# One stage for the reload and the first latent states, states between z products, row groups by halves at a tile's end

## What is computed

```python
def ssd_scan(xh, bm, cm, dt_raw, a_log, dt_bias, h0, reverse, with_output):
    dt = jax.nn.softplus(dt_raw + dt_bias.reshape(SSD_GROUPS, SSD_HPG))
    a_cum = jnp.cumsum(dtc * a, axis=2)
    decay_to_end = jnp.exp(a_cum[:, :, -1:] - a_cum)
    states = jnp.einsum("bcsgn,bcsgrp->bcgrpn", bc, (decay_to_end * dtc)[..., None] * xc)
    h = chunk_decay * h + states            # chunk after chunk

def peer(h, w_q, sub_keys, u_tab, v_tab):
    # per token and head: the 16 best of 128 x 128 experts, with softmax gates
    act = jax.nn.gelu(jnp.einsum("tkd,td->tk", u_tab[it], xt))
    return jnp.einsum("tk,tkd->td", gt * act, v_tab[it])
```

## Time and profile before

| | us |
|---|---|
| median of 3 runs | 4668.28 (4664.34 to 4676.31) |
| the profiled execution | 4667.22, its span 4665.4, mean granted clock of PE 0.865 |
| context peer, first to last dots | 391.9 to 1149.7 |
| reload; first latent states; outputs begin | 1161.7; 1211.9; 1242.3 |
| latent peer of layer 0 | 1456.8 to 2852.6 |
| projection of layer 1; its states; outputs begin | 2863; 3009.0; 3033.0 |
| last peer | 3335.3 to 4651.9 |

### The profile page before, as it was taken

How to read it: one execution, slowest core, us unless ns; L and a number is a source line. 1 busy time by engine, 2 the same in 40 slices (tenths; PEclk the granted TensorE clock), 3 DMA queues, 4 the chain that set the end, 5 groups by cost and what they waited for, 6 DMA issues and landing times. The chain is left out here.

```text
span 4665.4 us, 48881 instructions
## 1 busy us (share of the span) xinstructions
PE 3434.4 (74%) x15768; PEld 1728.3 (37%) x15768; DVE 3191.9 (68%) x6618; ACT 1543.8 (33%) x3799; POOL 2058.5 (44%) x1555
## 2 busy tenths in 40 slices
PE   7898889897799886555777557888997555655554
PEld 6586224332575333111333114767632111111111
DVE  5465887664766767766766776686666677777775
ACT  4442344343442225222222323474222222222221
POOL 0173444543123554555444551034355555555554
PEclk9899999999899989777789788999998777777778
DMA  5647999999647999999999995263699999999998
GB/s 212 218 158 298 410 410 395 420 423 393 232 161 272 422 417 398 409 421 421 398 425 425 391 412 211 101 204 109 236 423 413 416 412 423 414 408 414 411 418 361
DMA packets 276276, 1622.97 MB, mean 348 GB/s; under 512 B 47074, under 2 KB 61218, under 8 KB 87717
## 3 DMA queue, kind: packets, MB, share of 16 engines
q0 software_dynamic: 184320, 1342.26, 69.6%
q1 hardware_dynamic: 91700, 277.59, 16.3%
HBM read 1598.40 MB, written 21.33 MB: 347 GB/s over the span
## 5 line engine op out<-in xcount | busy, mean ns | idle before, releaser
L2727 PE MATMUL banks<-arena 128*64 128x512 f32 x5120 | 1569.3, 748 | 1003.2 <-ACT arena L2483 1001.8
L2193 POOL DMA_INDIRECT arena<-in_experts,arena x1280 | 1527.0, 1193 | 1660.0 <-PE banks L2727 1408.3
L2316 DVE CUSTOM_DVE_ANT_0 arena<-arena,token_copies 128x1024 f32<-128x1024 f32 x1280 | 1638.4, 1297 | 741.7 <-DMA arena<-in_experts,arena 681.6
L2727 PEld LDWEIGHTS banks<-arena 128*64 128x64 f32 x5120 | 377.1, 163 | 1983.4 <-ACT arena L2483 1357.0
L2476 ACT ACTIVATE arena<-arena 128x2 f32<-128x2 f32 x640 | 131.2, 205 | 1747.2 <-DVE arena L2316 1746.1
L2483 ACT ACTIVATE arena<-arena 128x64 f32<-128x64 f32 x1280 | 376.0, 340 | 298.8 <-POOL arena L2014 257.9
L303 POOL TENSOR_TENSOR wide_low<-wide_blocks,wide_high 128x1024 fp32r<-128x1024 f32 x88 | 219.1, 2513 | 277.7 <-ACT wide_high L292 233.3
L2540 PE MATMUL banks<-arena,wide_blocks 128*128 128x512 f32 (+3 forms) x960 | 307.0, 467 | 3.5 <-ACT arena L2345 2.1
L1025 POOL TENSOR_TENSOR arena<-arena 128x1024 f32<-128x1024 f32 x20 | 43.3, 2191 | 530.4 <-POOLq L853 479.5
L2617 PE MATMUL banks<-arena,wide_blocks 128*128 128x512 f32 x576 | 277.2, 619 | 0.0
L347 PE MATMUL banks<-activation_a,wide_high 128*128 128x256 f32 (+1 forms) x768 | 255.9, 333 | 23.8 <-DVE arena L1462 10.4
(11 more groups left out here) (268 smaller groups left out, 4789.0 us busy)
## 6 DMA issues: line engine op xcount, KB each, us to landing
wide_blocks<-in_wide SPq DMA_DIRECT2D x186, 1024.0 KB, 6.0
arena<-cum_rows SPq DMA_DIRECT2D x80, 256.0 KB, 3.8
arena<-in_experts,arena POOLq DMA_INDIRECT x1280, 11.1
pre_scan<-arena SPq DMA_DIRECT2D x16, 256.0 KB, 7.3
arena<-pre_scan SPq DMA_DIRECT2D x16, 256.0 KB, 5.2
residual<-in_tokens SPq DMA_DIRECT2D x6, 512.0 KB, 6.4
arena<-mod_rows SPq DMA_DIRECT2D x6, 512.0 KB, 8.5
norm_rows<-in_keys SPq DMA_DIRECT2D x3, 1024.0 KB, 6.5
```

Of the source, the lines that this page charges most:

```text
L2193: pool.indirect_dma_start(out=v.ring[:, g % RING], out_offset=None, in_=io["experts"], in_offset=bass.IndirectOffsetOnAxis(ap=c.idx[:, u % ...
L2316: last = nc.vector.tensor_tensor_reduce(out=u_row, in0=u_row, in1=k.copies[:, n % NJ], scale=1.0, scalar=0.0, op0=ALU.mult, op1=ALU.add, a ...
L2727: mm = nc.tensor.matmul(k.ps[j * QUAD:(j + 1) * QUAD, a + half], v.lhs[:, g % 4, j], v.ring[:, (g * NJ + j) % RING, D + half * BANK:D + (h ...
```

## The change

**Reload and states become one stage,** `stage_reload_states`. The modulation products come in two rounds of four. DVE's order becomes biased, box 0, steps, boxes 1 and 2, rests, joins 0 and 1, box 3, weights, joins 2 and 3, then state 0, joins 4 and 5, state 1, joins 6 and 7, states 2 to 5. PE has state(n) and modulation products between its mixes. The z rows are loaded near the end, and the first gate of the outputs stage waits for them. Buffers move to make room.

**`stage_project` has `inside=True` for layer 1's latent tokens:** dt products after product 1, the fold after 3, the decay sums after 9, their transposes after 13, the other decay steps between convolutions; the six states run after each of the first six z products; the unit decays stand behind the last z silu. `stage_states(1, LATENT)` is gone.

**In the peer stages** the last unit of a tile (but not of the stage) and the first unit of the next have their 16 rows in another order: the eight rows of half 0, then the eight of half 1. That is 14 units at seven boundaries. The next tile's copies for half 0 are made after the fourth pair of the last unit, those for half 1 after the eighth.

```diff
+            if inside:
+                load_wides(k, sp, w0 + 8 + WIDE_SLOTS)
+                sp.wait_ge(k.cum_moved.sem, k.cum_moved.at(1))
+                sp.dma_start(io["cum"].rearrange("t r c -> r t c")[:, 0:NT], cum_rows).then_inc(k.cum_kept.sem, 16)
+                sp.wait_ge(k.cum_kept.sem, kept0 + 16)
+                for n in range(4):
+                    load_sums(k, sp, after, n, 0, 0, n)
...
+                if inside and m == 1:
+                    dt_products()
+                if inside and m == 3:
+                    dt_fold()
+                if inside and m == 9:
+                    decay.sums(pe)
+                if inside and m == 13:
+                    turn_sums()
+            if not inside:
+                dt_products()
...
+                if n < len(steps):
+                    state(n)
+            if inside:
+                pe.wait_ge(k.state_added.sem, k.state_added.at(len(steps)))
+                products_bc(k, v, 0, 6)
...
+                if inside and m == 2:
+                    move_dt()
+                if inside and m == 4:
+                    copy_dt()
+                if inside and m == 6:
+                    decay.logs(act)
+                if inside and m == 12:
+                    decay.decays(act)
...
+            if inside:
+                act.wait_ge(k.cum_turned.sem, k.cum_turned.at(1))
+                nc.scalar.copy(cum_rows, k.ps[0:32, 6, 0:T].rearrange("p (t c) -> p t c", t=NT)).then_inc(k.cum_moved.sem, 1)
+            else:
...
+            if inside:
+                for n in range(EARLY_UNITS):
+                    unit_decays(k, act, after, n, 0, 0, n, row0)
...
+                if inside and m == 5:
+                    dve.wait_ge(k.dt_copied.sem, k.dt_copied.at(1))
+                    decay.biased(dve)
+                if inside and m == 7:
+                    decay.steps(dve)
+                if inside and m == 10:
+                    decay.rests(dve)
+                if inside and m == 13:
+                    decay.weights(dve)
...
+            if inside:
+                dve.wait_ge(k.turn_copied.sem, k.turn_copied.at(X_TILES + B_TILES))
+                dve.drain()
+                scale_x(0)
+                cut(9)
+                dve.wait_ge(k.silu_done.sem, k.silu_done.at(SCAN_TILES))
+                for n in range(len(steps)):
+                    state(n)
+                    if n in (1, 3):
+                        cut(10 + n // 2)
+                return
...
-            for m in range(8):
-                sp.dma_start(sig[:, m], io["pre_gp"][m]).then_inc(k.reloaded[3].sem, 16)
+            gate_rows(0)
+            gate_rows(1)
             for m in range(B_TILES):
                 sp.dma_start(v.CT[:, m], io["pre_scan"][X_TILES + B_TILES + m]).then_inc(k.reloaded[2].sem, 16)
-            for b in range(4):
-                for pair in range(2):
-                    sp.dma_start(v.zs[:, 2 * pair:2 * pair + 2, b * WIDE:(b + 1) * WIDE],
-                                 io["pre_z"][2 * b + pair].rearrange("p (t c) -> p t c", t=2)).then_inc(k.reloaded[2].sem, 16)
-            def store(m):
-                sp.wait_ge(k.part_ready.sem, k.part_ready.at(m + 1))
-                sp.dma_start(io["pre_part"][m], part[:, m % 2]).then_inc(k.part_kept[m % 2].sem, 16)
-
-            for m in range(8):
-                store(m)
-            sp.wait_ge(k.reloaded[2].sem, C + 16 * (B_TILES + 8))
+            mods.load(sp, 0)
+            wides(1)
+            sp.wait_ge(k.cum_moved.sem, k.cum_moved.at(1))
+            sp.dma_start(io["cum"].rearrange("t r c -> r t c")[:, 0:NT], cum_rows).then_inc(k.cum_kept.sem, 16)
+            store(0)
+            store(1)
+            gate_rows(2)
+            gate_rows(3)
+            wides(2)
+            wides(3)
+            sp.wait_ge(k.cum_kept.sem, kept0 + 16)
+            sp.wait_ge(k.mixed_ready.sem, k.mixed_ready.at(4))
+            for m in range(4, 8):
+                gate_rows(m)
+            for n in range(4):
+                load_sums(k, sp, v, n, 0, 0, n)
+            store(2)
+            store(3)
+            wides(4)
+            wides(5)
+            store(4)
+            store(5)
+            mods.keep(sp, 0)
+            mods.load(sp, 1)
+            z_rows(0)
+            store(6)
+            store(7)
             for i in range(2):
                 sp.wait_ge(k.part_kept[i].sem, k.part_kept[i].at(64))
+            z_rows(1)
+            wides(count)
+            mods.keep(sp, 1)
...
+            mods.take(act, 0)
             decay.decays(act)
+            act.wait_ge(k.cum_turned.sem, k.cum_turned.at(1))
+            nc.scalar.copy(cum_rows, k.ps[0:32, 5, 0:SEQ].rearrange("p (t c) -> p t c", t=NT)).then_inc(k.cum_moved.sem, 1)
+            for i in range(1, count + 1):
+                mods.take(act, i)
+                if i == 4:
+                    act.wait_ge(k.yp_proj.sem, k.yp_proj.at(8))
+                    unit_decays(k, act, v, 0, 0, 0, 0, row0)
+                if i == 5:
+                    unit_decays(k, act, v, 1, 0, 0, 1, row0)
...
+            box(0)
+            decay.steps(dve)
+            box(1)
+            box(2)
+            decay.rests(dve)
+            join(0)
+            join(1)
+            box(3)
+            decay.weights(dve)
+            join(2)
+            join(3)
+            dve.wait_ge(k.turn_copied.sem, k.turn_copied.at(X_TILES))
+            dve.drain()
+            scale_x(0)
+            state(0)
+            join(4)
+            join(5)
+            state(1)
             join(6)
             join(7)
...
+    def row_of(u, n):
+        border = (u % PEER_HEADS == 0 and u) or (u % PEER_HEADS == PEER_HEADS - 1 and u < UNITS - 1)
+        return (n % RANKS, n // RANKS) if border else (n // NJ, n % NJ)
+
+    def first_of_half(u, n):
+        return all(row_of(u, x)[1] != row_of(u, n)[1] for x in range(n))
+
+    def last_of_half(u, n):
+        return all(row_of(u, x)[1] != row_of(u, n)[1] for x in range(n + 1, TOPK))
...
-    copy_at = lambda n: FIRST + 13.0 + 3.0 * n if n < 2 * NJ else dot_at(n // (2 * NJ) * PEER_HEADS * TOPK - 1) + 5.0
+    copy_at = lambda n: (FIRST + 13.0 + 3.0 * n if n < 2 * NJ else
+                         dot_at(n // (2 * NJ) * PEER_HEADS * TOPK - 1 - (RANKS if n // 2 % NJ == 0 else 0)) + 5.0)
...
-                            in_offset=bass.IndirectOffsetOnAxis(ap=c.idx[:, u % 4, n // NJ, n % NJ:n % NJ + 1], axis=0),
+                            in_offset=bass.IndirectOffsetOnAxis(ap=row_index(u, n), axis=0),
...
-                        if u % PEER_HEADS == 0 and n < NJ:
-                            dve.wait_ge(k.copy_ready.sem, k.copy_ready.at(t * 2 * NJ + 2 * n + 2))
+                        j = row_of(u, n)[1]
+                        if u % PEER_HEADS == 0 and first_of_half(u, n):
+                            dve.wait_ge(k.copy_ready.sem, k.copy_ready.at(t * 2 * NJ + 2 * j + 2))
...
-                            out=u_row, in0=u_row, in1=k.copies[:, n % NJ], scale=1.0, scalar=0.0,
+                            out=u_row, in0=u_row, in1=k.copies[:, j], scale=1.0, scalar=0.0,
...
-                            act.wait_ge(k.dots.sem, b0["dots"] + t * PEER_HEADS * RANKS)
+                            act.wait_ge(k.dots.sem, b0["dots"] + t * PEER_HEADS * RANKS - (RANKS // 2 if j == 0 else 0))
...
-                    if u % PEER_HEADS == PEER_HEADS - 1 and t + 1 < NT:
-                        yield from copies(t + 1)
+                        if u % PEER_HEADS == PEER_HEADS - 1 and t + 1 < NT and q % (RANKS // 2) == RANKS // 2 - 1:
+                            yield from copies(t + 1, [q // (RANKS // 2)])
...
+                                n = q * NJ + j
+                                part = row_of(u, n)[1]
                                 mm = nc.tensor.matmul(
-                                    k.ps[j * QUAD:(j + 1) * QUAD, a + half], v.lhs[:, g % 4, j],
+                                    k.ps[part * QUAD:(part + 1) * QUAD, a + half], v.lhs[:, g % 4, j],
                                     v.ring[:, (g * NJ + j) % RING, D + half * BANK:D + (half + 1) * BANK],
-                                    start=(first and q == 0), stop=(final and q == RANKS - 1), skip_group_check=True)
+                                    start=(first and first_of_half(u, n)), stop=(final and last_of_half(u, n)),
+                                    skip_group_check=True)
...
+                        if final and t + 1 < NT and q == RANKS // 2 - 1:
+                            yield from copies(t + 1, [0])
...
-                            yield from copies(t + 1)
+                            yield from copies(t + 1, [1])
```

295 lines of the change are left out of this document (222 added, 73 removed).

## The result

| | us |
|---|---|
| median before / after, 4 runs each | 4668.23 / 4699.43 |
| ratio, 95% interval | 1.0075 [1.0058, 1.0093] |
| the profiled execution after | 4707.19, its span 4705.2, mean granted clock of PE 0.878 |
| forecast | 4650.0, range 4630 to 4674 |

The account below looks back on a forecast made before the run. Peer stages, two thirds of the span, were taken as bound by DMA gathers with PE in the loop, DVE or PE bounding between them. Terms -7 - 9 - 2 = -18 on 4667.2 give 4649.2, median 4650, range 4630 to 4674.

Parts of the forecast that it names:

- Row groups by halves: Peer stages' seven tile boundaries: earlier copies gain, serial passes cost, together -2 us, bounds -14 to +14.
- The price of a serial pair: Border units: eight passes of a pair on the same PE columns take 3.70 us instead of 1.94, +1.76 per pair.
- The cushion: Peer tile ends: rows in flight cover DVE's 10.87 us wait except about 5, leaving about 6 of slack.
- The context: Context peer's boundary: 28 us of PE work added against 11 idle; after 5 recovered and 3.6 caught up, +8.
- The gain of early copies: Tile boundaries: 5 us recovered in the context's, 10 together at the other six; bounds for all seven 5 and 35.
- rival 2: Border units of the peer stages: all serial passes are hidden, -18 there, total 4633 us; chance 0.17.
- The reload's sum: Fused reload and first states: 12.8 us of DVE idle removed, less a new stall of 5.8, gives 7 us; bounds 0 to 14.
- stall: Fused reload stage: DVE waits 5.8 us before join(6) until store(4) has left the buffer.
- the landing of a store: Fused reload stage: 2.0 us until the store has landed, part of the 9.4 us chain ahead of join(6).
- The projection: Second layer's projection: states between z products let the outputs begin at 3023.9 instead of 3032.95, 9 us gained; bounds 3 to 14.
- Rival 1: Latent peers' twelve border units: PE paces them at the lower clock, total 4734 us; decided by over 30 net; chance 0.08.
- The signs: For wrong: border passes in 1.9 us, DMA shares below 0.9 in non-context border units, or DVE waiting on z rows.

Follow-up runs that it names:

- The two fillers: Kernel before, with four more PE products per pair in the 14 border units (eight in the context), behind or ahead of the slots' release: 4694.97 and 4725.51 us.
- serial_only: Kernel before, with only the border units' row products of each pair sent to the same half of the PSUM partitions: 4722.06 us against 4662.53.
- copies_early: Kernel before, rows in old order, with only PE's copies of the next tile into PSUM moved ahead of and right behind the last pair: 4660.89 against 4664.48.
- stages_only: The whole change without the new row order in the peer stages, against the kernel before: 4653.60 us against 4662.53, ratio 0.9979.

## Why the prediction was wrong

**The step that failed** is in "Row groups by halves": "In the last peer PE is busy 810 of 1316.6 us [...], so a unit of 16 rows [...] has 15.8 idle: it fits, barely, and costs nothing in my sum." The price of a serial pair was right (3.65 measured, 3.70 taken), and so was its place. What was wrong is that idle time on PE was counted as cover. PE's idle time before these products is time in which it waits for ACT, which waits for the next pair's dots (1001.8 of 1003.2 us before the change); it lies ahead of each pair, not behind it. A pair that takes longer (1.8 at full clock, 1.2 on the mean at the end looked at) frees its two slots that much later whatever PE's share of idle time, and the gathers behind them are issued later. The row for this was in my first paragraph: 1408.3 of POOL's 1660.0 idle are for PE. The two fillers show it: the same work on PE, behind the release +29, ahead of it +63.

**The cushion** was overrated with it. I took the rows in flight (11.1 us to land) as slack that a late release does not touch, and from 10.87 of wait and 5 of loss at one boundary a cushion of 6. In the last peer, where the old copies left DVE waiting 5.6 to 8.3 us, the DMA share over the two units stayed at 0.99 to 1.00; sixteen late pairs, each about 1.1 us later than before (61.4 us for the sixteen instead of 44.0 at the first end), took it to 0.96 or 0.97 in serial_only, which lost 2.9 to 3.4 a boundary. So a single gap is covered and a row of late releases is not, wholly. My reading is that the cushion is not refilled while the transfers are the bound; no run tests that.

**The context** was priced at +8 and its two units grew by 12.6; the same happened in the first boundary of layer 0 (+11.6), which I had counted among those where PE is idle. It lies where the woven projection ends. A mean over the last peer (0.62 busy) was applied to stretches that it doesn't describe. In place of -2, the part cost about +50 alone, and +59.5 without what the early copies give.

**The gain of early copies** was about right in size: 15 were forecast (5 + 10), and 9.5 and 17 measured. (The prediction is not at one with itself here: serial passes hidden everywhere are -14 in the part's bounds and -18 in rival 2; its own terms give -15.) But most of the first boundary's bubble came from PE's copies standing late in its queue, which I had read in the order of instructions and not priced: copies_early gets it without touching a row.

**The fused stages.** The reload's sum had the right mechanism, and its stall was mis-sized: 7.66 instead of 5.8, and a second one of 3.22 before join 4, where stores 2 and 3 stand behind gates and sums on SP, and PE's of 7.52 behind keep(0). The term that was off is the landing of a store. The 2.0 of the earlier trace rows is a median over a queue in which, for the last six of its eight stores, nothing else was issued. In the fused stage store 4 was issued 4.8 us after the scaling began (1223.73), sooner than the 7.4 of the sum, and took 6.0 to land. And I had followed one semaphore through SP's queue and not all of the stores. -3 to -4 instead of -7. The projection came out at 9.5 for 9.05, with its tail on ACT as worked out. Together -9 was measured (stages_only, -5 to -15 by its interval) for -16: right in sign, over by about 7, of which the reload accounts for 3 to 4. The outputs stages behind don't account for the rest, since they are as long in kernels without the fusing. For the Trainium skill's drain of the table load ("ScalarE: Activation LUTs", What ACT_TABLE_LOAD costs) there was again no room: 3049.33 to 3054.46, 5.1 us for both unit decays.

**The rivals.** Rival 1 had the place and the sign, and 4734 for 4699; its point of decision (30 us over seven boundaries; it was 49) was usable. Its condition, the lower clock, was not what decided: the granted clock in the two units shown rose from 0.66 and 0.76 to 0.85 and 0.88. I gave it 0.08 because "PE has 38% idle there", the same error. The fact in the prediction's first paragraph, that POOL waits for PE, should have made it the likeliest case.

**The signs** didn't catch it. None of those named for "wrong" came: a border pair took 3.65 and not 1.9, the DMA share over the two units at each end was 0.94 to 0.98, and DVE waited for no z rows. The case in which the passes are serial as priced and still cost time had no sign of its own.

**The rule against the change.** The Trainium skill ("TensorE: Matmul & The Clock Gate", Part 3: Packing small matmuls) has small products run at the same time in different tiles of the array. The trace agrees: 1.94 for a pair in different halves, 3.65 in the same one. As I used it, it lowered the price; as a warning against giving up the packing it was the most useful sentence at hand.

## What to carry to other kernels

Idle time of an engine is no cover for work that is put ahead of its signal. Ask what the engine releases and who is waiting for that; if a resource ring bounded by DMA hangs on the release, work ahead of it costs (here 60 us for 112 pairs), and the same work behind the release costs less (30), or nothing where the engine has room. Before regrouping work so that a dependent step can start early, see whether the step is late only because of where it stands in a static queue. Before a difference of 2 or 3 us between two traces is called an effect, look at the same stretch in other traces of the old code. And where one queue carries stores that free buffers beside loads that wait for others, follow each store through it, not the first one.
